# Hybrid decoder layer on one core: attention of every prompt tile inside the main slots of the mixer, gram tiles on both sides of the first inverse, the output turned in another PSUM bank

## What is computed

```
h = rmsnorm(x, g_pre_mix) * (1 + scale_m) + shift_m
xc, z, b_lg, a_lg, q_b, k_b, v_b = split(h @ w_in)
qa, ka, va = split(silu(causal_conv(xc, conv_w)))          # 4 heads x 128
# group A, gated delta rule: S_t = a_t S_{t-1}(I - b_t k_t k_t^T) + b_t v_t k_t^T, o_t = S_t^T q_t
o_a = rmsnorm(o_a, gdn_norm_w) * silu(z)
# group B: attention of 8 query heads x 64 over a window of 128, 2 kv heads, a learned sink per head
mix = concat(o_a, o_b) @ w_o
x = x + gate_m * rmsnorm(mix, g_post_mix)
y = square(relu(h2 @ w_up)) @ w_down
x = x + gate_f * rmsnorm(y, g_post_ffn)
```

## Time and profile before

| what | us |
|---|---|
| median of 3 runs (3108.83 to 3113.99) | 3108.84 |
| the profiled execution | 3114.03 |
| its span | 3112.3 |
| PE busy in the span | 2766.7 (89%) |
| DVE busy | 1481.7 (48%) |
| ACT busy | 867.4 (28%) |
| mean granted TensorE clock | 0.932 |

### The profile page before, as it was taken

How to read it: one execution, slowest core, us unless ns; L and a number is a source line. 1 busy time by engine, 2 the same in 40 slices (tenths; PEclk the granted TensorE clock), 3 DMA queues, 4 the chain that set the end, 5 groups by cost and what they waited for, 6 DMA issues and landing times. The chain is left out here.

```text
span 3112.3 us, 45866 instructions
## 1 busy us (share of the span) xinstructions
PE 2766.7 (89%) x18510; PEld 2421.8 (78%) x18510; DVE 1481.7 (48%) x2020; ACT 867.4 (28%) x1632; POOL 307.3 (10%) x417
## 2 busy tenths in 40 slices
PE   4999999975748768699799999999988999999996
PEld 2998989973426556588689889898878989988995
DVE  2646464725556555345444444444454444344444
ACT  2434343322334314233322112121123112211211
POOL 1111111110001111111100000000005000000003
PEclk6999999996869768699899999999999999999998
DMA  6554545434237334445421101011034101110113
GB/s 216 155 161 153 153 144 150 149 100 149 58 94 207 106 111 118 133 146 178 128 83 54 52 29 54 27 54 54 27 95 153 55 27 54 54 52 29 54 54 108
DMA packets 354373, 309.39 MB, mean 99 GB/s; under 512 B 41970, under 2 KB 308511, under 8 KB 354232
## 3 DMA queue, kind: packets, MB, share of 16 engines
q1 hardware_dynamic: 341208, 263.86, 29.0%
q0 software_dynamic: 13040, 43.81, 4.1%
HBM read 235.86 MB, written 72.70 MB: 99 GB/s over the span
## 5 line engine op out<-in xcount | busy, mean ns | idle before, releaser
L81 PE MATMUL up_ps<-h_hi,w_up_hi 128*128 128x264 f32 (+1 forms) x2048 | 580.3, 283 | 19.8 <-DVE h_lo L2762 12.4
L82 PE MATMUL up_ps<-h_lo,w_up_hi 128*128 128x264 f32 (+1 forms) x2048 | 583.3, 285 | 0.0
L83 PE MATMUL up_ps<-h_hi,w_up_lo 128*128 128x264 f32 (+1 forms) x2048 | 580.6, 283 | 0.0
L2784 DVE TENSOR_TENSOR y<-y,down_ps 128x1024 f32<-128x1024 f32 (+1 forms) x272 | 332.1, 1221 | 315.8 <-PE down_ps L83 315.3
L81 PE MATMUL down_ps<-w_down_hi,u_hi 128*128 128x512 f32 x1088 | 433.4, 398 | 18.2 <-issue 9.7
L83 PE MATMUL down_ps<-w_down_hi,u_lo 128*128 128x512 f32 x1088 | 429.7, 395 | 0.0
L82 PE MATMUL down_ps<-w_down_lo,u_hi 128*128 128x512 f32 x1088 | 427.7, 393 | 0.0
L81 PE MATMUL proj_ps<-h_hi,w_in_hi 128*128 128x262 f32 x1408 | 407.3, 289 | 16.7 <-DVE h_lo L656 13.5
L81 PEld LDWEIGHTS up_ps<-h_hi,w_up_hi 128*128 128x128 f32 x2048 | 389.3, 190 | 22.6 <-issue 13.8
L82 PE MATMUL proj_ps<-h_lo,w_in_hi 128*128 128x262 f32 x1408 | 402.5, 286 | 0.0
L83 PE MATMUL proj_ps<-h_hi,w_in_lo 128*128 128x262 f32 x1408 | 402.1, 286 | 0.0
(11 more groups left out here) (490 smaller groups left out, 3765.2 us busy)
## 6 DMA issues: line engine op xcount, KB each, us to landing
w_in_raw<-in_w_in SPq DMA_DIRECT2D x88, 512.0 KB
w_up_raw<-in_w_up SPq DMA_DIRECT2D x66, 512.0 KB
w_down_raw<-in_w_down SPq DMA_DIRECT2D x64, 512.0 KB, 4.7
proj_scratch<-chunk_out POOLq DMA_DIRECT2D x88, 256.0 KB, 3.6
w_ada_cols<-in_w_ada SPq DMA_DIRECT2D x8, 2048.0 KB, 9.2
qkv<-proj_scratch SPq DMA_DIRECT2D x16, 768.0 KB, 6.0
p_w_ada_cols<-in_w_ada SPq DMA_DIRECT2D x4, 2048.0 KB, 15.2
prep_qk<-proj_scratch SPq DMA_DIRECT2D x16, 512.0 KB, 4.3
```

What stands on the lines that cost most here:

```text
L81: nc.tensor.matmul(out, whi, mhi, start=first, stop=False)
L82: nc.tensor.matmul(out, whi, mlo, start=False, stop=False)
L83: return nc.tensor.matmul(out, wlo, mhi, start=False, stop=last)
L2784: v.tensor_tensor(acc, acc, pd[r, (par * H.tiles + t) % 2], ALU.add).then_inc(H.s_y, 1)
```

## The change

- `slots` has 9 slots ahead of the main tiles. Slots 0 to 3 make gram tiles 0 to 7, slots 4 to 6 invert the first group, slot 7 makes gram tiles 8 and 9, slot 8 makes 10 and 11, readies main tile 0 and takes the scores of attention tile 0. Main slot t takes the scores of attention tile t + 1 and the rest of tile t; gram tiles 12 to 15 are made in main slots 0 and 1; the second inversion is cut in five, in main slots 2 to 6 (parts 0, 1, 2, 3, and 4 with 5).
- Gram tiles 0 and 1 take their decays from SBUF, with 4 f32 matmuls, and no longer wait for the split rows that go through DRAM.
- The sample's first step goes behind the tables of decays on PE, ACT and DVE, and into banks 3 and 4. Its state (2 MB) is loaded two slots later.
- `turn_out` writes bank 1. It waits for the next tile's scaled v instead of `state`, and the wait of `against_state` for `out_gate` moves to `turn` and `prep`.
- In a slot, PE's second `scores` stands right behind `out_state`, `attn_out` ahead of `level_y64`, `turn_out` behind it. On DVE the second `maxes` stands right behind `state`, `out_norm` ahead of the first `probs`, `place_z32` ahead of `out_scale`. On ACT `square_o` stands ahead of the second copy of probabilities.

```
 def slots():
+    plan = [(None, None, (2 * i, 2 * i + 1), None, None, None) for i in range(4)]
+    plan += [(None, None, (), None, None, (0, 0, 2)), (None, None, (), None, None, (0, 2, 4)), (None, None, (), None, None, (0, 4, 6)),
+             (None, None, (8, 9), None, None, None), (None, 0, (10, 11), 0, None, None)]
+    preps = {0: (12, 13), 1: (14, 15)}
+    fwd = {2: (1, 0, 1), 3: (1, 1, 2), 4: (1, 2, 3), 5: (1, 3, 4), 6: (1, 4, 6)}
     for t in range(NT):
+        nxt = t + 1 if t + 1 < NT else None
+        plan.append((t, nxt, preps.get(t, ()), nxt, t, fwd.get(t)))
...
-                def prep(t, mps):
+                def prep(t, mps, main):
...
+                    if t >= 2:
+                        mm(dp[:, 0, :], ones3[:], grp[:, p], start=True, stop=False)
+                    else:
+                        for h in range(HA):
+                            mm(dp[:, 0, h * P:(h + 1) * P], gg[:, t, h:h + 1].broadcast_to([P, P]), k["ut"][:], start=(h == 0), stop=False)
...
+                        if half == 0 and main:
+                            pe.wait_ge(s_oa, main)
...
                 def turn(t, preps):
...
+                    if t > 1:
+                        pe.wait_ge(s_oa, t - 1)
...
                 def against_state(t):
...
                         pe.wait_ge(s_st, t)
-                        pe.wait_ge(s_oa, t)
...
                 def turn_out(t):
                     pe.wait_ge(s_on, t + 1)
-                    pe.wait_ge(s_st, t + 1)
+                    pe.wait_ge(s_vs, min(t + 2, NT))
                     for h in range(HA):
-                        last = tr(dp[:, 3, h * P:(h + 1) * P], on[:, h, :], ident[:])
+                        last = tr(dp[:, 1, h * P:(h + 1) * P], on[:, h, :], ident[:])
```

More of the change, by code:

```diff
@@ L918, in sample_pe @@
     yield
-    A, B = banks
     for n in range(2):
@@ L1108, in sample_act, with sample_dve @@
     yield
-def sample_dve(nc, dve, k, S, first, banks):
+def sample_dve(nc, dve, k, S, A, B):
     v = nc.vector
@@ L1732, in _ @@
                         out_state(t)
+                    if a is not None:
+                        scores(a, 1)
                     if b is not None:
@@ L1735, in _ @@
                     for j in preps[1:2]:
-                        prep(j, mps)
+                        prep(j, mps, t)
+                    if t is None:
+                        next(sample, None)
                     if mp is not None:
@@ L1740, in _ @@
                         turn_probs(b, 2)
-                    if t is None:
-                        next(sample, None)
-                    if a is not None:
-                        scores(a, 1)
                     if mp is not None:
@@ L1773, in _ @@
                 a.activation(ax[:], ax[:], ACT.Exp, scale=-1.0).then_inc(s_act0, 1)
-                sample = sample_act(nc, act, k, S, dp[:, 3, :], dp[:, 4, :])
-                next(sample)
                 act.wait_ge(s_act0, 3)
@@ L1780, in _ @@
                 a.activation(dk[:], dk[:], ACT.Exp).then_inc(s_act0, 1)
+                sample = sample_act(nc, act, k, S, dp[:, 3, :], dp[:, 4, :])
+                next(sample)
                 act.wait_ge(s_pre, 9)
@@ L1875, in _ @@
                         exps(n, 0)
+                    if t is None:
+                        next(sample, None)
+                    if t is not None:
+                        square_o(t)
                     if b is not None:
                         read_probs(b, 1)
-                    if t is None:
-                        next(sample, None)
                     for j in preps[1:2]:
                         decay(j)
-                    if t is not None:
-                        square_o(t)
-                    else:
+                    if t is None:
                         next(sample, None)
@@ L1912, in _ @@
                 v.tensor_tensor(ax[:], xa[:], na[:], ALU.max).then_inc(s_pre, 1)
-                sample = sample_dve(nc, dve, k, S, (dp[:, 0, :], dp[:, 1, :]), (dp[:, 3, :], dp[:, 4, :]))
-                next(sample)
                 v.tensor_copy(identb[:], k["ident"][:])
@@ L1951, in _ @@
                 v.tensor_tensor(nfac[:], ncol[:], dk[:], ALU.mult).then_inc(s_pre, 1)
+                sample = sample_dve(nc, dve, k, S, dp[:, 3, :], dp[:, 4, :])
+                next(sample)
                 dve.wait_ge(s_pre, 10)
@@ L2131, in _ @@
                         decayed(j)
+                    if t is None:
+                        next(sample, None)
+                    if n is not None:
+                        maxes(n, 1)
                     if mp is not None:
                         scale_k(mp)
+                    if t is not None:
+                        out_norm(t)
                     if n is not None:
                         probs(n, 0)
-                    if t is not None:
-                        out_norm(t)
-                    else:
-                        next(sample, None)
                     if mp is not None:
                         scale_qk(mp)
+                    if mp is not None:
+                        place_z32(mp)
                     if t is not None:
@@ L2144, in _ @@
                     if n is not None:
-                        maxes(n, 1)
-                    if mp is not None:
-                        place_z32(mp)
+                        probs(n, 1)
                     if t is not None:
                         out_gate(t)
-                    if n is not None:
-                        probs(n, 1)
                     if mp is not None:
```

50 lines of the change are left out of this document (18 added, 32 removed), and 3 rows, old and new, of the table plan.

## The result

The changed kernel takes 2995.6 us (median of 4 runs, 2993.8 to 2998.1) against 3109.2 before: a ratio of 0.963 (95% interval 0.962 to 0.964), 113.6 us less. The forecast was 3025, the range 2985 to 3062. The profiled execution took 2993.8 (span 2992.0), that of before 3114.0 (span 3112.3), so between the two traces there are 120.2 us to explain.

A forecast was written before the change was run, and what follows sets the result against it. It took chains between engines, not one engine, to bound the kernel. Its terms, -14 - 24 - 31 - 25 + 8 + 2 = -84, took the profiled 3114.0 us to 3030, so 3025 for the median; range 2985 to 3062.

The forecast's parts named there:

- the main tiles: All 16 main tiles: 366.5 us against 364.7, +2, while taking in eight more attention tiles.
- the front: Stages ahead of the main tiles, from the start to main tile 0: -86 us in sum.
- the start: Up to the first gram tile, its decays now from SBUF: -14 us, ends -10 and -16.
- slots 4 and 5: Slots 4 and 5 up to the inversion, as attention work leaves: -31 us, ends -24 and -36.
- the slot with attention: A main slot with attention: 20.3 us, ends 18.5 and 23.7, with 1 us added for a lower clock.
- Slots 0 to 3: Slots ahead of the main tiles that attention tiles 0 and 1 leave: -24 us, ends -20 and -31.
- the way to main tile 0: From the first inverse to main tile 0, gets longer through SP's queue in order: +8 us, ends -2 and +20.
- the second inversion: Its five pieces in main slots 2 to 6: 22.6 us of waits, plus 9 for lower clock, ends 0 and 19.
- Rival 1: Main slots with attention don't get shorter, since DVE steps queue behind the second maxes: +30 us, 3055; chance 0.20.
- rival 3: PE falls to the lower clock level and stays there in the main slots: +204 us, 3229; chance 0.04.
- Rival 2: The front gains more, in slots 0 to 5 and before main tile 0: -22 us, 3003; chance 0.10.
- The first inversion: 58.5 us become its own 31.1 plus 2.5 for the sample's steps: -25 us, ends -20 and -27.

The follow-up runs named there:

- e8_kept_busy: Changed kernel with matmuls that nobody reads put ahead of `new_v` in main slots 3 to 7, to fill PE's waits; 2988.6 us.
- e3_bank3: Changed kernel with the output's turn in bank 3 again, so that `against_state` waits for `out_gate`; 2998.1 us.
- e5_rows_early: Changed kernel with the 24 stores of the sample's rows issued during the first inversion, no more ahead of main tile 0's loads; 2995.8 us.
- e10_pe_tail_order: Changed kernel with the end of PE's slot in the old order: output's turn, 64-level, then the attention's product; 3041.8 us.
- e2_late_maxes: Changed kernel with DVE's second maxes put back between `scale_qk` and `place_z32`, not behind `state`; 3017.1 us.
- e9_front_loads: Changed kernel with the sample's rows stored and attention tile 0 loaded during the first inversion; 2986.1 us.
- e6_w_o_early: Changed kernel with the output projection's weights loaded over eight slots in place of one burst from the last slots; 2993.0 us.
- e7_both_early: Changed kernel with the sample's rows stored during the first inversion and the output projection's weights loaded over eight slots; 2992.6 us.
- e11_dram_rows: Changed kernel with the decays of gram tiles 0 and 1 through DRAM and the split rows, as before; 3004.3 us.
- e1_old_plan: Changed kernel with the slots' plan of before and attention tile 0 loaded first; new orders, bank 1 and new start stay; 3070.3 us.
- e4_three_slots: Changed kernel with the second inversion in three slots of two parts each (main slots 2 to 4) in place of five slots; 2992.3 us.
- e12_all_together: Changed kernel with second inversion in three slots, filling matmuls, sample's rows and attention tile 0 early, and projection weights over eight slots; 2972.6 us.

## Why the prediction was right, and where it was off

**The argument held.** Attention tiles were dear ahead of the main tiles and cheap in them; the plan moved eight of them. Sign, place and order of the stages came out as said, and the sum of the front, -86 forecast, was -98.3, or -92.9 without the 5.4 us ahead of the mixer. In the traces the forecast missed by 36.2 us (3030 against 2993.8): -12.3 in the front, -32.9 in the main tiles and +9.0 behind them. Three terms fell outside the ends stated for them (the start, -20.9 against -16, though 5.4 of it are not the change's; slots 4 and 5, -38.8 against -36; the slot with attention, 17.96 us against 18.5), so the total is in the range by the width of the whole, not because each term was bounded well. Of the signs named, main tile 0 began at 835.6 us, 12 earlier than said and within the limits given.

**Slots 0 to 3** (-24, measured -24.7), **the way to main tile 0** (+8, measured +7.3) and **the second inversion** (22.6 + 9, measured 33.2 over five slots) were right in size. The waits of `new_v` forecast as 6, 4, 3, 1 and 7 us were 6.3, 5.7, 3.8, 1.7 and 7.6. The 9 us for the clock behind them were 8.1 by the slots and 7.9 by e8_kept_busy; the forecast had put 3 us on three waits, and all five paid 1.2 to 2.4. In the change each of the five waits brought the granted clock down, even that of 1.7 us (0.92 in slot 6), but at 1.2 to 2.4 us and not at the 3.8 each that the earlier trace rows gave. By the rule weighed there, of the Trainium skill ("TensorE: Matmul & The Clock Gate", "HAM oscillation — how this bites in real kernels"), each recurring long gap sends the array back to half clock. The trace of the change agrees for the long waits; to count all five was the working's own step beyond that page, and with the waits a little shorter it does not hold: those of 3.02 and 0.88 us in slots 5 and 6 of e3_bank3 left the clock at 1.00.

**The way to main tile 0 was right for the wrong step.** The working summed SP's queue, with 7.9 us for the sample's rows, as the path. e5_rows_early took these away and nothing moved: the path went through PE's wait for attention tile 0, a load queued behind SP's wait for gram tile 9. The working had named that load only as 2 us extra; PE waits 8.02 us for it in the change. Two chains of about the same length stood there: taking the rows off one gave 0.3 us, shortening both gave 8.1.

**The slot with attention failed**: 20.3 us forecast, less than 18 called what "cannot be had", and 17.96 measured. Over the 13 slots with full attention and no grams that is 30 us of error; slots 12 and 14 with a lower clock and the second inversion take 5 of it back, slots 0 and 1 (49.3 us for 53) and slot 15 (13.9 for 18) add 8, which makes the 33 us by which the main tiles were wrong. Two steps of that working were false. "PE is busy 18.5 us of the old slot, so less than 18 cannot be had" took busy time for a constant of the work. It had 1.2 us or more of lower clock in it (seven products with `attn_v` in 3.13 us, where eight take 1.94), and that clock came back with the waits gone; e10_pe_tail_order shows that one such wait brings it down. And "I add 1 us" for the clock counted in the wrong direction: with its waits gone, the slot has the clock back. Taking away the 2.7 us of waits gave 2.7 us and some 0.8 to 1 of clock on top; e10_pe_tail_order put one wait of 2 us back and lost 3.1 to 4.5 a slot. The forecast also gave DVE's second maxes the larger share (the 1.73 us); e2_late_maxes puts 1.5 us on them, and the place of the attention's product on PE is worth twice as much.

**Rival 1** (slots that don't get shorter) is refuted by the windows above, **rival 3** (PE stays at the lower clock) too: slot 8 was back at 1.00 right behind the longest wait. **Rival 2** (the front gains more) came true beside the forecast: of its 22 us 9.2 came, 7.8 of them in slots 4 and 5.

**The front's terms.** The start was forecast at -14 with -16 as its far end, and it was -20.9. Of that, 5.4 us are chance ahead of the mixer, and the change's own 15.5 lie within the ends. The sample's first step does stand in front of the first gram tile on PE, as the working had it (its last matmuls begin at 697.35 us, the spreading of the decays at 697.71). What it left out is that the same step stood ahead of `g_all` on DVE before, 2.6 us. Slots 4 and 5 gave 38.8 for 31: only PE's times and waits for attention were counted, while in the trace of before DVE's maxes and probabilities also stand ahead of the sample's state updates; that this is the difference was read from the trace, and no run tests it. The first inversion took 37.3 us and not 33.6: 4.4 us of state updates on DVE (`w_o_raw`, 16 of 0.28 us) and 1.7 us of waits for them lie between its first two parts, in place of the 2.5 us left for the sample.

**Nothing was forecast behind the mixer**, and 9 us were given back there: 6.1 up to the first product of the projection, most of them by its own loads, and 2.9 in the rest, which is no more than this stretch varies. The working asked what each moved step delays inside the mixer, but not what the next stage's prefetch collides with once the last main tile is shorter.

## What to carry to other kernels

A wait of a microsecond or two in a loop on TensorE may cost its length twice: read the granted clock and the mean time of the matmuls behind it before you take an engine's busy time as a floor. The cheapest cure is an independent, long product of another chain put where the wait is; where there is none, matmuls that nobody reads bought 7.9 us over five slots here. When a stage gets shorter, look at the prefetch for the next one that was timed by it, and at loads with a free buffer that stand behind a wait in a queue that is served in order.

## What the runs showed of the hardware that was not expected

The granted clock fell in slots in which PE waited for nothing longer than 0.4 us. Main slots 12 and 14 of the change take 19.7 us at 0.91, slots 10, 11 and 13, with the same instructions and the same short waits, 17.9 or 18.0 at 1.00. The fall lies in the same place each time, the attention's product, whose eight matmuls go from 605 to 1030 or 1045 ns (means), and it comes in every second slot: 12 and 14 in the change, 8, 10 and 12 in e5_rows_early and e9_front_loads, 8, 10, 12 and 14 in e6_w_o_early and e7_both_early, 10, 12 and 14 in e8_kept_busy, and 8, 10, 12 and 14 in e11_dram_rows. Slot 12 of e1_old_plan is such a one, too. In slots 6 to 14 of e4_three_slots and e12_all_together there is none, with the same slots, but slot 3 of e12_all_together falls at this product; in e3_bank3, with a wait of 0.8 us more in each slot and thus a longer slot, there is none either, and in e2_late_maxes one. What decides it was not settled. It moves the time of such a kernel by up to 7 us without any change in the slots themselves, more than several of the edits here.

Nor does the length of a wait decide alone. A wait of 0.8 us in each slot left the clock at 1.00 in slots 8 to 14 of e3_bank3 and in all but one of e2_late_maxes, and one of 2.0 us (e10_pe_tail_order) brought it down in every slot. But waits of 2.33 us (slot 6 of e2_late_maxes) and 3.02 us (slot 5 of e3_bank3) ahead of `new_v` left it at 1.00, while one of 1.67 us in the same place (slot 6 of the change) came with 0.92. Why was not settled.
